# A decoder trunk on one core: the third block sum of each seven-product unit made by an adding transfer instead of by VectorE

## The chip, the cores and the metric

The kernel runs on one core of a Trainium2 chip. The metric is the device time of one execution in microseconds (us), given as the median of several runs. The engines of the core are TensorE (PE in the profile, with its weight loads as PEld), VectorE (DVE), ScalarE (ACT), GpSimd (POOL) and SyncE (SP), and 16 DMA engines move data between the device memory and the on-chip memory.

## The reference

The input is a sequence of 256 tokens of width 1024 in float32. Two layers each do

```python
xn = rms_norm(h, norm_mix_g[layer])
...
h = h + mix
hn = rms_norm(h, norm_ffn_g[layer])
h = h + (silu(hn @ ffn_w_gate[layer]) * (hn @ ffn_w_up[layer])) @ ffn_w_down[layer]
```

The first layer's `mix` is a causal pooling mixer beside differential attention, the second's a convolution module beside block attention. A last RMS norm ends the trunk. `ffn_w_gate` and `ffn_w_up` are 1024 x 2816 and `ffn_w_down` is 2816 x 1024. What matters here is the product of `hn` with the two up matrices.

## The kernel before

**Weights.** Every weight is stored in the device memory as slabs of 128 x 2048 float32 (1 MB). SP loads a slab in two halves (`load`, L488 to L495) into one of five buffers `raw`, or for some slabs into `spare`. The products are made to float32 precision from float32r parts: ACT writes the high part `w_hi` (a copy, L632, or L949 for a slab that is a sum), DVE writes the low part `w_lo = raw - w_hi` (L1120), and PE then runs three matmuls with 512 columns for each 128 x 512 piece: high by high, low input by high weight, high input by low weight. `w_hi` and `w_lo` have six slots (`SLOTS`). A prepared slab may overwrite a slot only when PE has released it (`slab_used`).

**The order.** No scheduler is at work: each engine runs a list that is written out by hand. The function `places` (L81 to L155) sets the order in which slabs are loaded (`loads`) and prepared (`preps`), and which buffer each uses; `next_hi` on ACT and `next_lo` on DVE take the next slab of `preps`.

**The feed-forward stage.** Its 2816 columns are eleven chunks of 256. Six pairs of chunks, at 3, 6 and 8 in each layer (`SEVEN_AT`), are done as seven-product units (Strassen's scheme in Winograd's form), so that seven block products do the work of eight. The four weight blocks of a unit are B11, B12, B21 and B22. Beside B11, B21 and B22 themselves the unit needs four sums of blocks:

- T3 = B12 + B22, held in the buffer y: POOL issues an adding transfer of 1 MB (`add_third`, L600 to L605), which reads B22 from the device memory and adds it into y, where B12 lies. Its semaphore is `third_added`.
- T2 = B11 - T3, held in x, where B11 lay: DVE, `block_add(a, 0)`.
- T1 = T2 + B22, held in y: DVE, `block_add(a, 1)`.
- T4 = T2 + B21, held in x: DVE, `block_add(a, 2)`, with B21 in the buffer e.

All three of DVE are one instruction of 128 x 2048 at L1682, and their semaphore is `block_sum`. A sum may overwrite its buffer only when both parts of what lay there have been taken (`lo_ready` of that slab).

A unit prepares its slabs in the order b11, t3, t2, a down slab, t1, b21, b22, t4, a down slab, and PE uses them in that order (`seven` of the tensor block, L2331 to L2367; a product with a sum is at L2323, L2324 and L2328). Between the products ACT copies partial results out of the PSUM banks (`seven_copy`, L982): the third of these copies reads the result of the t1 product, and PE waits for it before the b22 product. DVE adds it in (`seven_add`, L1690) and, some instructions later, makes the low part of the first turned activation (`seven_act_lo`, L1705), which PE waits for before the down product (L1832 and after).

**POOL.** Its list is short: constants, thirteen small powers for the norms (L615), and after the powers of the feed-forward norm of each layer the three adding transfers of that layer's units, one behind the other.

Of the kernel before, what the change touches and what calls it, by code (L numbers as in the profile page):

```python
# [37 lines left out]
ALU = mybir.AluOpType  # L38
# [24 lines left out]
NAT = (4, 5)  # L63
NCH = 11
SEVEN_AT = ((3, 6, 8), (3, 6, 8))
WHOLE = [("block", l, a + 1, 1) for l in range(2) for a in SEVEN_AT[l]]
SPARE = RAW_SLOTS
EARLY = SPARE + 1

# [11 lines left out]
def places():  # L81

    loads, preps, place = [], [], {}
    counts = [0] * (EARLY + 1)
    freed = {r: (0, []) for r in range(RAW_SLOTS)}
    units = 0

    def load(key):

        n = len(loads)  # L90
        r = min(freed, key=lambda q: freed[q][0])
        _, waits = freed.pop(r)
        counts[r] += 16 if FIRST_SLABS <= n < PARTED else 16 * LOADS
        loads.append((key, r, waits))
        return r, counts[r]

    def prepare(key, r, made):
        place[key] = len(preps)
        preps.append((r, made))

    def free(r, *more):

        freed[r] = (len(preps), [("lo", len(preps))] + list(more))

    def slab(key):
        r, made = load(key)
        prepare(key, r, made)
        if r != EARLY:
            free(r)

    for l in range(2):
        place["mix", l] = len(preps)
        for n in range(NAT[l] + 6):
            slab(("mix", l, n))
        place["out", l] = len(preps)
        for n in range(4):
            slab(("out", l, n))
        spare = [("lo", place["down", 0, NCH - 2] + 1)] if l else []
        for i in range(NCH):
            if i in SEVEN_AT[l]:  # L120
                if i == SEVEN_AT[l][0]:
                    freed[SPARE] = (len(preps) + 1, spare + [("forms", l + 1)])
                x, x_made = load(("block", l, i, 0))
                y, y_made = load(("block", l, i + 1, 0))
                z, z_made = load(("block", l, i + 1, 1))
                d, d_made = load(("down", l, before(l, i)))
                prepare(("b11", l, i), x, x_made)
                prepare(("t3", l, i), y, None)
                prepare(("t2", l, i), x, None)
                prepare(("down", l, before(l, i)), d, d_made)  # L130
                free(d)
                e, e_made = load(("block", l, i, 1))
                place["raw", l, i] = ((x, x_made), (y, y_made), (z, z_made), (e, e_made))
                prepare(("t1", l, i), y, None)
                free(y)
                d, d_made = load(("down", l, i + 1))
                prepare(("b21", l, i), e, e_made)
                prepare(("b22", l, i), z, z_made)
                free(z)
                free(e, ("sum", 3 * units + 3))  # L140
                prepare(("t4", l, i), x, None)
                free(x)
                prepare(("down", l, i + 1), d, d_made)
                free(d)
                units += 1
                continue
            if i - 1 not in SEVEN_AT[l]:
                for n in range(2):
                    slab(("up", l, i, n))
                if i:  # L150
                    slab(("down", l, before(l, i)))
        slab(("down", l, NCH - 1))
        freed.pop(SPARE, None)
        place["end", l] = len(preps)
    return loads, preps, place  # L155
# [13 lines left out]
def trunk(nc, x, x_cols, norm_mix_g, norm_ffn_g, norm_final_g, params_in, slabs, out):  # L169
# [45 lines left out]
    with ctx:  # L215
# [125 lines left out]
        raw_loaded = [sem(f"raw_loaded{i}") for i in range(EARLY + 1)]  # L341
        block_sum = sem("block_sum")
        third_added = sem("third_added")
        low_copied = sem("low_copied")
        x_kept = sem("x_kept")
        forms_made = sem("forms_made")
# [90 lines left out]

            return 4 * (st - 1) + 2 * half + b

        SUMS = ("t2", "t1", "t4")  # L440
        sum_of_prep = {}
        for l in range(2):
            for a in SEVEN_AT[l]:
                sum_of_prep[place["t3", l, a]] = (third_added, 16 * seven_no(l, a) + 16)
                for n, name in enumerate(SUMS):
                    sum_of_prep[place[name, l, a]] = (block_sum, len(SUMS) * seven_no(l, a) + n + 1)
        LOW_AT = [[i for i in range(2, NCH - l) if not in_seven(l, i)] for l in range(2)]
# [39 lines left out]
        def _(sp):  # L487
            def load(n):  # L488

                key, r, free = loads[n]  # L490
                for what, count in free or ():
                    sp.wait_ge({"lo": lo_ready, "forms": forms_ready, "sum": block_sum}[what], count)
                for b in range(2):
                    c = slice(b * SLAB // 2, (b + 1) * SLAB // 2)
                    sp.dma_start(raw_of(r, c), piece(n, c.start, c.stop)).then_inc(raw_loaded[r], 16)  # L495
# [73 lines left out]
        @block.gpsimd  # L569
        def _(pool):  # L570
            made = [0]

            def step(ins):

                made[0] += 1
                ins.then_inc(consts, 1)
                pool.wait_ge(consts, made[0])

            step(nc.gpsimd.memset(power[:, :], -0.5))
            step(nc.gpsimd.memset(ident[:, :], 0.0))  # L580
            step(nc.gpsimd.affine_select(out=ident[:, :], in_=ident[:, :], compare_op=ALU.not_equal, fill=1.0,
                                         base=0, pattern=[[-1, P]], channel_multiplier=1))
            assert made[0] == IDENT_MADE
            step(nc.gpsimd.tensor_copy(ident_b[:, :], ident[:, :]))
            step(nc.gpsimd.memset(mask_b[:, :, :], 0.0))

            step(nc.gpsimd.affine_select(out=mask_b[:, :, :], in_=mask_b[:, :, :], compare_op=ALU.is_ge, fill=NEG,
                                         base=0, pattern=[[0, 4], [-1, P]], channel_multiplier=1))
            pool.wait_ge(cols_lo, KC)


            step(nc.gpsimd.memset(u_in[:, :, 0:UPAD], 0.0))
            for g, w in enumerate(POOL_WINDOWS):
                r = slice(64 * (g % 2), 64 * (g % 2) + 64)
                step(nc.gpsimd.memset(per_count[r, g // 2, :], 1.0 / w))
                for t in range(w - 1):
                    step(nc.gpsimd.memset(per_count[r, g // 2, t:t + 1], 1.0 / (t + 1)))
            assert made[0] == CONSTS_MADE

            def add_third(l, a):  # L600

                y, made = place["raw", l, a][1]
                n = [key for key, _, _ in loads].index(("block", l, a + 1, 1))
                pool.wait_ge(raw_loaded[y], made)
                nc.gpsimd.dma_start(raw_of(y), piece(n, 0, SLAB), accum_op=ALU.add).then_inc(third_added, 16)  # L605

            for n, (kind, a, b) in enumerate(POWS):
                pool.wait_ge(pow_asked, n + 1)
                if kind == "norm":
                    o, i, e = rstd[:, b:b + 1], meansq[:, b:b + 1], power[:, 0:1]  # L610
                elif kind == "head":
                    o, i, e = osq[:, :], osq[:, :], power[:, :]
                else:
                    o, i, e = rstd[:, 2:4], meansq[:, 2:4], power[:, 0:2]
                nc.gpsimd.tensor_tensor(o, i, e, ALU.pow).then_inc(pow_done, 1)  # L615
                if (kind, a, b) in (("norm", 1, 1), ("norm", 3, 1)):
                    for unit in SEVEN_AT[a // 2]:
                        add_third(a // 2, unit)


        @block.scalar
# [484 lines left out]
        def _(dve):  # L1106
# [431 lines left out]
            def ffn_dve(l):  # L1538
# [131 lines left out]
                def block_add(a, m):  # L1670

                    raws = place["raw", l, a]
                    for r, made in ((raws[0],), (raws[2],), (raws[3],))[m]:
                        dve.wait_ge(raw_loaded[r], made)
                    dve.wait_ge(lo_ready, place[("b11", "t3", "t2")[m], l, a] + 1)
                    if m == 0:
                        dve.wait_ge(third_added, 16 * seven_no(l, a) + 16)
                    else:
                        dve.wait_ge(block_sum, 3 * seven_no(l, a) + m)
                    x, y, z, e = (raw_of(r) for r, _ in raws)  # L1680
                    o, p, q = ((x, x, y), (y, z, x), (x, e, x))[m]
                    V.tensor_tensor(o, p, q, ALU.add if m else ALU.subtract).then_inc(block_sum, 1)  # L1682

                def seven_add(a, m):
# [22 lines left out]
                def seven(a):  # L1707
# [3 lines left out]
                    if follows:  # L1711
                        seven_act_lo(a - 2, 3)
                        block_add(a, 1)
                        block_add(a, 2)
                        next_lo()
                    else:
                        next_lo()
                        block_add(a, 2)
                    next_lo(2)
                    if follows:  # L1720
                        seven_add(a, 0)
                        next_lo()
# [778 lines left out]
```

## Time and profile before

| | |
|---|---|
| time of three runs | 559.43, 559.46, 559.73 us; median 559.46 |
| span of the profiled execution | 557.6 us |
| granted clock of TensorE over the span | 0.998 |
| PE, DVE, ACT, POOL busy | 551.2, 467.6, 341.3, 20.4 us |
| adding transfers issued by POOL | 6 of 1 MB |

The profiled execution comes with its span alone, from its first instruction to its last. The median of the timed runs is 1.9 us longer than this span; it is what lies around the span. A matmul's end is modelled in the trace, so PE rows overlap: in a run of matmuls with 512 columns the next one starts every 0.23 us, while each row shows about 0.39 us.

The layers' units stand at these places of the span: unit 3 of layer 0 with its PE products from 146 us, unit 6 from 193 us, unit 8 from 224 us, and in layer 1 from 421, 468 and 499 us.

### The profile page before, as it was taken

Reading aid. Unit: us, or ns where it says so; the run is one execution under the profiler, and the core shown is the slowest. Engines: PE = TensorE matmul, PEld = TensorE weight load, DVE = VectorE, ACT = ScalarE, POOL = GpSimd, SP = SyncE. Lnnn points to the kernel's source line nnn. Section 1 sums busy time; section 2 is a strip of 40 time slices with the busy share of each in tenths; the row PEclk is TensorE's granted clock in tenths of the full one; section 3 lists DMA queues with packets and bytes.
Section 4 is the critical chain, followed back from the end, with each engine's and each line's share of the span. In section 5 each row is a group of like instructions: output and inputs, shape, how many; then the busy total and the mean of one; then the engine's idle time right before and its main releaser. Section 6 shows DMA issues by size and latency. Waiting matters only on the chain.

```text
span 557.6 us, 7496 instructions
## 1 busy us (share of the span) xinstructions
PE 551.2 (99%) x2877; PEld 468.8 (84%) x2877; DVE 467.6 (84%) x562; ACT 341.3 (61%) x471; POOL 20.4 (4%) x60
## 2 busy tenths in 40 slices
PE   9999999999999999999999999999999999999996
PEld 8899988888888888888888888888888888888885
DVE  5779996788996997997798998977889889979875
ACT  6778664756664773666566366647387557656724
POOL 1200001000000000000000000000000000000000
PEclk9999999999999999999999999999999999999999
DMA  8995544474379259277469422444916790773502
GB/s 300 409 401 199 185 150 152 150 216 163 121 277 336 97 182 343 78 285 290 148 253 366 168 75 76 156 147 158 306 64 224 287 320 21 222 286 143 197 1 75
DMA packets 31429, 111.95 MB, mean 201 GB/s; under 512 B 3489, under 2 KB 4641, under 8 KB 30625
## 3 DMA queue, kind: packets, MB, share of 16 engines
q1 hardware_dynamic: 30384, 105.04, 50.2%
q0 software_dynamic: 864, 6.29, 5.8%
q8 instruction: 23, 0.38, 0.3%
q10 hardware_dynamic: 144, 0.14, 0.1%
q14 instruction: 14, 0.11, 0.1%
HBM read 110.40 MB, written 1.05 MB: 200 GB/s over the span
## 4 chain that ended last, share of the span: by engine, by line
PE 99%; DVE 0%; DVEq 0%; issue 0%; ACT 0%; ACTq 0%
PE bank L1834 16%; PE bank L1832 16%; PE bank L1833 16%; PE bank L2277 8%; PE bank L2324 7%; PE bank L2328 7%; PE bank L2323 7%; PE bank L2282 4%; PE bank L1943 4%; PE bank L1946 2%; PE bank L1896 1%; PE bank L1893 1%; PE bank L1889 1%; PE bank L1915 1%; PE bank L2289 1%; PE bank L2035 1%
## 5 line engine op out<-in xcount | busy, mean ns | idle before, releaser
L1120 DVE TENSOR_TENSOR w_lo<-raw,w_hi 128x2048 fp32r<-128x2048 f32 (+2 forms) x98 | 217.2, 2232 | 18.2 <-ACT w_hi L632 16.7
L632 ACT ACTIVATE w_hi<-raw 128x2048 fp32r<-128x2048 f32 (+2 forms) x81 | 149.5, 1861 | 11.4 <-PE bank L1834 7.4
L1832 PE MATMUL bank<-w_lo,yT_hi 128*128 128x512 f32 (+1 forms) x242 | 96.5, 399 | 0.0
L1834 PE MATMUL bank<-w_hi,yT_lo 128*128 128x512 f32 (+1 forms) x242 | 94.1, 389 | 0.0
L1833 PE MATMUL bank<-w_hi,yT_hi 128*128 128x512 f32 (+1 forms) x242 | 94.0, 388 | 0.0
L1834 PEld LDWEIGHTS bank<-w_hi,yT_lo 128*128 128x128 f32 x242 | 45.4, 188 | 9.6
L1832 PEld LDWEIGHTS bank<-w_lo,yT_hi 128*128 128x128 f32 x242 | 45.5, 188 | 8.4 <-DVE yT_lo L1335 0.2
L1833 PEld LDWEIGHTS bank<-w_hi,yT_hi 128*128 128x128 f32 x242 | 45.6, 188 | 8.2
L2277 PE MATMUL bank<-xT,w_hi 128*128 128x512 f32 x192 | 48.5, 394 | 0.0
L949 ACT ACTIVATE w_hi<-raw 128x2048 fp32r<-128x2048 f32 x24 | 45.8, 1910 | 2.9 <-DMA raw<-in_slabs 2.6
L1832 PE MATMUL bank<-w_lo,xT 128*128 128x512 f32 (+1 forms) x112 | 42.8, 382 | 0.0
L1834 PE MATMUL bank<-w_hi,xT 128*128 128x512 f32 (+1 forms) x112 | 42.1, 376 | 0.0
L1833 PE MATMUL bank<-w_hi,xT 128*128 128x512 f32 (+1 forms) x112 | 42.0, 375 | 0.0
L2277 PEld LDWEIGHTS bank<-xT,w_hi 128*128 128x128 f32 x192 | 34.7, 189 | 6.4
L2323 PE MATMUL bank<-w_hi,forms_hi 128*128 128x512 f32 x96 | 37.5, 391 | 0.0
L2324 PE MATMUL bank<-w_hi,forms_lo 128*128 128x512 f32 x96 | 37.4, 390 | 0.0
L1682 DVE TENSOR_TENSOR raw<-raw 128x2048 f32<-128x2048 f32 x14 | 32.0, 2289 | 0.7
L2323 PE MATMUL bank<-w_hi,xT 128*128 128x512 f32 x72 | 28.6, 397 | 0.0
L2324 PE MATMUL bank<-w_hi,xT 128*128 128x512 f32 x72 | 28.1, 390 | 0.0
L2282 PEld LDWEIGHTS bank<-xT,w_lo 128*128 128x128 f32 x192 | 26.2, 190 | 1.9
L1832 PE MATMUL bank<-xT,w_hi 128*128 128x256 f32 x96 | 27.6, 287 | 0.0
L1834 PE MATMUL bank<-xT,w_lo 128*128 128x256 f32 x96 | 27.2, 283 | 0.0
(247 smaller groups left out, 973.3 us busy)
## 6 DMA issues: line engine op xcount, KB each, us to landing
raw<-in_slabs SPq DMA_DIRECT2D x170, 512.0 KB, 4.8
spare<-in_slabs SPq DMA_DIRECT2D x16, 512.0 KB, 7.0
raw<-in_slabs POOLq DMA_DIRECT2D x6, 1024.0 KB, 9.7
raw<-in_slabs SPq DMA_DIRECT2D x5, 256.0 KB, 4.3
h<-in_x SPq DMA_DIRECT2D x2, 512.0 KB, 7.1
early<-in_norm_ffn_g SPq DMA_DIRECT2D x2, 512.0 KB, 10.1
raw<-in_slabs SPq DMA_DIRECT2D x6, 128.0 KB, 4.6
h<-in_x_cols SPq DMA_DIRECT2D x1, 512.0 KB, 5.5
```

What stands on the lines that cost most here:

```text
L632: A(w_hi[:, s % SLOTS, c], raw_of(r, c), ACT.Copy).then_inc(hi_ready, 1)
L949: A(w_hi[:, slot(ahead[0]), :], raw_of(r), ACT.Copy).then_inc(hi_ready, 1)
L1120: V.tensor_tensor(w_lo[:, s % SLOTS, c], raw_of(preps[s][0], c), w_hi[:, s % SLOTS, c].bitcast(F32), ALU.subtract).then_inc(lo_ready, 1)
L1682: V.tensor_tensor(o, p, q, ALU.add if m else ALU.subtract).then_inc(block_sum, 1)
L1832: T.matmul(o, st_hi, mv_lo, start=first, stop=False, skip_group_check=onto)
L1833: T.matmul(o, st_hi, mv_hi, start=False, stop=False, skip_group_check=onto)
L1834: return T.matmul(o, st_lo, mv_hi, start=False, stop=last, skip_group_check=onto)
L2277: T.matmul(bank[:, b + m, :], hi, xT[:, k, :, :, :], start=k == 0, stop=False)
L2282: last = T.matmul(bank[:, b + m, 0:SEQ], lo, xT_hi[:, :, k, :], start=False, stop=k == KC - 1)
L2323: T.matmul(bank[:, b, :], hi[:, k, :], w1, start=not onto and k == 0, stop=False, skip_group_check=onto)
L2324: T.matmul(bank[:, b, :], lo[:, k, :], w1, start=False, stop=False, skip_group_check=onto)
L2328: last = T.matmul(bank[:, b, :], hi[:, k, :], w2, start=False, stop=k == n - 1, skip_group_check=onto)
```

## The change

T4 is no longer made by DVE. POOL gets a second adding transfer for each unit, `add_fourth`: it reads B21 from the device memory and adds it into x, where T2 lies. B21 is now stored in the device memory row by row over its whole width, as B22 is (`WHOLE`), and is still loaded to e for its own product. ACT's high part of T4 waits for `fourth_added`. `block_add(a, 2)` and its place in DVE's list go, and the load that reuses e no longer waits for the sum.

```diff
-WHOLE = [("block", l, a + 1, 1) for l in range(2) for a in SEVEN_AT[l]]
+WHOLE = [("block", l, a + b, 1) for l in range(2) for a in SEVEN_AT[l] for b in range(2)]
...
-                free(e, ("sum", 3 * units + 3))
+                free(e)
...
-        SUMS = ("t2", "t1", "t4")
+        SUMS = ("t2", "t1")
...
+                sum_of_prep[place["t4", l, a]] = (fourth_added, 16 * seven_no(l, a) + 16)
...
+            def add_fourth(l, a):
+
+                x = place["raw", l, a][0][0]
+                n = [key for key, _, _ in loads].index(("block", l, a, 1))
+                pool.wait_ge(lo_ready, place["t2", l, a] + 1)
+                pool.wait_ge(block_sum, len(SUMS) * seven_no(l, a) + 2)
+                nc.gpsimd.dma_start(raw_of(x), piece(n, 0, SLAB), accum_op=ALU.add).then_inc(fourth_added, 16)
...
                         add_third(a // 2, unit)
+                        add_fourth(a // 2, unit)
...
                     if follows:
                         seven_act_lo(a - 2, 3)
                         block_add(a, 1)
-                        block_add(a, 2)
-                        next_lo()
-                    else:
-                        next_lo()
-                        block_add(a, 2)
-                    next_lo(2)
+                    next_lo(3)
```

Two places show how the lists change. The first is DVE in unit 8 of layer 0, where T1 and T4 were made back to back and the low parts of t1, b21 and b22 follow (`raw` and `spare` are the load buffers, `w_lo` the slots). Before:

```order
L1705 TENSOR_TENSOR yT_lo<-bank,yT_hi 128x256 [waits at_hi]
L1682 TENSOR_TENSOR raw<-spare,raw 128x2048 [waits block_sum,lo_ready,raw_loaded5]
L1682 TENSOR_TENSOR raw<-raw 128x2048 [waits block_sum,lo_ready,raw_loaded1]
L1120 TENSOR_TENSOR w_lo<-raw,w_hi 128x2048 [waits hi_ready] x2
L1120 TENSOR_TENSOR w_lo<-spare,w_hi 128x2048 [waits hi_ready]
L1690 TENSOR_TENSOR work<-bank,work 128x512 [waits seven_copied,slab_used]
```

And now:

```order
L1714 TENSOR_TENSOR yT_lo<-bank,yT_hi 128x256 [waits at_hi]
L1691 TENSOR_TENSOR raw<-spare,raw 128x2048 [waits block_sum,lo_ready,raw_loaded5]
L1129 TENSOR_TENSOR w_lo<-raw,w_hi 128x2048 [waits hi_ready] x2
L1129 TENSOR_TENSOR w_lo<-spare,w_hi 128x2048 [waits hi_ready]
L1699 TENSOR_TENSOR work<-bank,work 128x512 [waits seven_copied,slab_used]
```

One sum has left DVE's list and nothing else has moved. The second place is POOL's list in layer 0, from the unit 3 transfer to the next power. Before:

```order
L605 DMA raw<-in_slabs 128x2048 [waits raw_loaded3]
L605 DMA raw<-in_slabs 128x2048 [waits raw_loaded2] x2
L615 TENSOR_TENSOR rstd<-meansq,power 128x1 [waits pow_asked] x2
```

And now:

```order
L605 DMA raw<-in_slabs 128x2048 [waits raw_loaded3]
L613 DMA raw<-in_slabs 128x2048 [waits block_sum,lo_ready]
L605 DMA raw<-in_slabs 128x2048 [waits raw_loaded2]
L613 DMA raw<-in_slabs 128x2048 [waits block_sum,lo_ready]
L605 DMA raw<-in_slabs 128x2048 [waits raw_loaded2]
L613 DMA raw<-in_slabs 128x2048 [waits block_sum,lo_ready]
L623 TENSOR_TENSOR rstd<-meansq,power 128x1 [waits pow_asked] x2
```

The T3 transfer of the next unit now stands behind the T4 transfer of this one, which waits for DVE.

## Rows read from the trace of the kernel before

**Rows 1.** Page, busy us (share of the span) and instructions of each engine

```profile
PE 551.2 (99%) x2877; PEld 468.8 (84%) x2877; DVE 467.6 (84%) x562; ACT 341.3 (61%) x471; POOL 20.4 (4%) x60
```

**Rows 2.** Page, the chain that ended last: shares by engine

```profile
PE 99%; DVE 0%; DVEq 0%; issue 0%; ACT 0%; ACTq 0%
```

**Rows 3.** Waits of PE: engine, line, waited for: us in total, times, longest

```profile
PE bank L1828 <- DVE probT L1802: 1.0, 1, 1.0
```

**Rows 4.** DVE's timeline, unit 8 of layer 0: start, duration, instruction, [idle before]

```profile
229.51 2.29 DVE L1682 TENSOR_TENSOR raw<-spare,raw 128x2048 f32<-128x2048 f32 x1
231.93 2.29 DVE L1682 TENSOR_TENSOR raw<-raw 128x2048 f32<-128x2048 f32 x1
...
241.52 0.69 DVE L1690 TENSOR_TENSOR work<-bank,work 128x512 f32<-128x512 f32 x1
...
247.79 0.42 DVE L1705 TENSOR_TENSOR yT_lo<-bank,yT_hi 128x256 fp32r<-128x256 f32 x1
```

**Rows 5.** ACT's timeline, same unit: the high part of T4, the copy behind

```profile
238.38 1.90 ACT L949 ACTIVATE w_hi<-raw 128x2048 fp32r<-128x2048 f32 x1
240.64 0.60 ACT L982 ACTIVATE work<-bank 128x512 f32<-128x512 f32 x1 [0.35 <-PE bank L2328]
```

**Rows 6.** PE's timeline, same unit: first matmuls of b22 and down product

```profile
243.16 0.39 PE L2323 MATMUL bank<-w_hi,forms_hi 128*128 128x512 f32 x1
...
249.00 0.48 PE L1832 MATMUL bank<-w_lo,yT_hi 128*128 128x512 f32 x1
```

**Rows 7.** Adding transfers of POOL (L605): time from issue to landing

```profile
DMA to landing us min/median/max: 8.9/9.7/10.1
```

**Rows 8.** DMA queue of POOL, packets, MB, share: from 122 to 125 us

```profile
q0 software_dynamic: 78, 0.64, 102.7%
```

**Rows 9.** The same queue from 207 to 210 us, beside transfers of SP

```profile
q0 software_dynamic: 51, 0.42, 71.9%
```

**Rows 10.** Windows: us, PE, PEld, DVE, ACT, POOL busy, PEclk, DMA share, GB/s

```profile
241.52:248.21 6.69, 6.69 (x32) 5.49 (x32) 6.69 (x9) 5.08 (x6) 0.00 (x0) 1.00 0.80 302
205.00:206.50 1.50, 1.50 (x8) 1.27 (x7) 1.50 (x2) 0.76 (x1) 0.86 (x1) 1.00 0.00 0
233.60:238.40 4.80, 4.80 (x23) 3.94 (x22) 4.11 (x3) 4.80 (x4) 0.00 (x0) 1.00 0.03 5
238.60:240.00 1.40, 1.40 (x8) 1.14 (x7) 1.40 (x2) 1.40 (x1) 0.00 (x0) 1.00 0.91 354
```

**Rows 11.** Timelines of DVE, ACT and PE, unit 8 of layer 1

```profile
506.91 2.29 DVE L1682 TENSOR_TENSOR raw<-raw 128x2048 f32<-128x2048 f32 x1
...
513.32 1.90 ACT L949 ACTIVATE w_hi<-raw 128x2048 fp32r<-128x2048 f32 x1
...
523.93 0.48 PE L1832 MATMUL bank<-w_lo,yT_hi 128*128 128x512 f32 x1
```

**Rows 12.** Timelines of DVE and ACT, unit 3 of layer 0

```profile
144.70 2.28 DVE L1120 TENSOR_TENSOR w_lo<-raw,w_hi 128x2048 fp32r<-128x2048 f32 x1
...
154.87 1.92 ACT L949 ACTIVATE w_hi<-raw 128x2048 fp32r<-128x2048 f32 x1 [0.25 <-DVE raw L1682]
...
159.52 1.93 ACT L632 ACTIVATE w_hi<-raw 128x2048 fp32r<-128x2048 f32 x1 [0.93 <-PE bank L1834]
...
162.18 0.60 ACT L982 ACTIVATE work<-bank 128x512 f32<-128x512 f32 x1 [0.73 <-PE bank L2328]
```

**Rows 13.** Timelines of DVE, ACT, POOL: unit 6, and T3, T2 of unit 8

```profile
191.15 2.29 DVE L1120 TENSOR_TENSOR w_lo<-raw,w_hi 128x2048 fp32r<-128x2048 f32 x1
...
202.04 1.91 ACT L949 ACTIVATE w_hi<-raw 128x2048 fp32r<-128x2048 f32 x1
...
207.05 1.92 ACT L632 ACTIVATE w_hi<-raw 128x2048 fp32r<-128x2048 f32 x1 [1.29 <-PE bank L1834]
...
204.99 0.86 POOL L605 DMA_DIRECT2D raw<-in_slabs  x1 [32.48 <-DMA raw<-in_slabs]
...
219.11 2.28 DVE L1682 TENSOR_TENSOR raw<-raw 128x2048 f32<-128x2048 f32 x1
```

More of the change, by code:

```diff
@@ L85, in places @@
     freed = {r: (0, []) for r in range(RAW_SLOTS)}
-    units = 0
     def load(key):
@@ L144, in places @@
                 free(d)
-                units += 1
                 continue
@@ L343, in trunk @@
         third_added = sem("third_added")
+        fourth_added = sem("fourth_added")
         low_copied = sem("low_copied")
@@ L491, in load @@
                 for what, count in free or ():
-                    sp.wait_ge({"lo": lo_ready, "forms": forms_ready, "sum": block_sum}[what], count)
+                    sp.wait_ge({"lo": lo_ready, "forms": forms_ready}[what], count)
                 for b in range(2):
@@ L1672, in block_add @@
                     raws = place["raw", l, a]
-                    for r, made in ((raws[0],), (raws[2],), (raws[3],))[m]:
-                        dve.wait_ge(raw_loaded[r], made)
-                    dve.wait_ge(lo_ready, place[("b11", "t3", "t2")[m], l, a] + 1)
+                    r, made = raws[0] if m == 0 else raws[2]
+                    dve.wait_ge(raw_loaded[r], made)
+                    dve.wait_ge(lo_ready, place[("b11", "t3")[m], l, a] + 1)
                     if m == 0:
@@ L1678, in block_add @@
                     else:
-                        dve.wait_ge(block_sum, 3 * seven_no(l, a) + m)
-                    x, y, z, e = (raw_of(r) for r, _ in raws)
-                    o, p, q = ((x, x, y), (y, z, x), (x, e, x))[m]
+                        dve.wait_ge(block_sum, len(SUMS) * seven_no(l, a) + m)
+                    x, y, z, _ = (raw_of(r) for r, _ in raws)
+                    o, p, q = ((x, x, y), (y, z, x))[m]
                     V.tensor_tensor(o, p, q, ALU.add if m else ALU.subtract).then_inc(block_sum, 1)
```

## The prediction

> **What bounds the kernel now.** I read the busy times first: PE 551.2 us of a span of 557.6, DVE 467.6, and POOL, which gets the new work, 20.4 [rows 1]. Then the chain that ended last, which is PE for 99% and DVE for 0% [rows 2]. Since a busy PE could still be one that waits between matmuls, the list of PE's waits comes next: it holds one wait, of 1.0 us, at the very start of the kernel [rows 3]. So no wait for DVE stands in the 99%, and the question is only whether the new way of T4 puts one in. That is read from the timelines of DVE, ACT and PE around each T4 [rows 4 to 6, 11 to 13], and the duration of the new transfer from the six adding transfers that are there already and from what the DMA engines carry at the time [rows 7 to 10].
>
> **What is removed.** Six sums on DVE of 2.29 us [rows 4], 13.7 us of its 467.6. PE waits for DVE nowhere in the units, so this is worth 0 on the path. Its only trace should be low parts of b21, b22 and t4 made up to 2.3 us sooner in units 3 and 6; the high parts and PE's release of slots set the pace again behind them. SP's wait for the sum goes as well, but its other wait, for b22's low part, comes later than the sum in each unit: 0.
>
> **What is added.** Six transfers of 1 MB, each with this life: POOL issues it when T1 is made (units 8) or when t2's low part is made (units 3 and 6); it lands L us later; ACT, which works in order, takes T4's high part then. I need L and how late T4 may be.
>
> *The length L.* The six existing ones took 8.9 to 10.1 us [rows 7], all beside SP's traffic. With the DMA engines to itself such a transfer moves 0.64 MB in 3 us [rows 8], so 1.05 MB in 4.9 us; beside SP's loads it moves 0.42 MB in 3 us [rows 9], so it would take 7.5 us. Before the first packet there is a start-up: the transfer issued at 204.99 finds idle DMA engines, and nothing moves up to 206.50 [rows 10, 13], so at least 1.5 us; the longest landing less the slow transfer gives at most 10.1 - 7.5 = 2.6. I take 2.0. L lies between 1.5 + 4.9 = 6.4 and the 10.1 of the rows.
>
> The Trainium skill (DMA: Bandwidth & Descriptors, Anatomy of one DMA) puts a transfer issued by GpSimd at about 2.0 us plus its bytes by 436 KB per us. For 1 MB that is an estimate of 4.4 us, by which T4 would land before anyone asks and the sum would be 0 with room to spare; the rows have twice that for an adding transfer, and the rows decide.
>
> *Unit 8 of layer 0, the tight one.* T1 ends at 229.51 + 2.29 = 231.80 [rows 4]; POOL sees it about 0.1 later, as DVE did with its own T4 at 231.93. So the transfer is issued at 231.9, and its packets would run from 233.9. From 233.6 to 238.4 the DMA engines were idle (share 0.03), and at 238.6 SP's next slab begins (share 0.91) [rows 10]. The transfer is alone for 4.7 of its 4.9 us, and the rest at the slow rate costs 0.1 more: landing at about 239.0, **L = 7.1**. ACT asks for T4 at 238.38 [rows 5], so it gets it 0.6 us late.
>
> What stands behind that wait on ACT is the copy of t1's product at 240.64, which had 0.35 us of idle time ahead of it [rows 5]. Behind the copy stands DVE's add at 241.52: the copy ended at 241.24, so with 0.1 for the semaphore about 0.2 us are spare. From 241.52 to 248.21 DVE is busy without a gap [rows 10], up to the end of the low part that starts at 247.79 [rows 4], and PE wants that for its down product at 249.00 [rows 6]: 0.8, less 0.1 for the semaphore, 0.7 spare. Together T4 may be 0.35 + 0.2 + 0.7 = 1.25 us late before PE notices. In terms of L: ACT's request is 6.5 us after the issue, so **PE's stall is L - 7.7 us, and nothing below that**. The direct way, PE's wait for the copy before b22 at 243.16 [rows 6], has more room (copy done at 241.24, 1.8 spare after the 0.35). With L = 7.1 the stall is 0.
>
> *Unit 8 of layer 1.* The same distances: from DVE's old T4 at 506.91 to ACT's request at 513.32 are 6.41 us, and PE's down product follows 10.6 us after that [rows 11], as 10.6 in layer 0. Stall 0.
>
> *Units 3.* T2's low part ends at 146.98, so the issue is at 147.1 and T4 is asked for at 154.87 [rows 12]: 7.8 us. SP's loads come into it half way, so I take L = 8, late by 0.2. Even L = 10.1 makes it only 2.3 late, and ACT idles 0.93 and then 0.73 us for PE before the copy that matters [rows 12]; 0.6 remains, against the 1.8 of the direct way above. Stall 0.
>
> *Units 6.* Issue at 193.44 + 0.1, request at 202.04, 8.5 us; 1.6 late at worst, and 1.29 us of idle time for PE come behind it [rows 13]. Stall 0.
>
> *The queues.* POOL's list is passed in order, so the T3 transfer of the next unit waits for the issue of T4's. That of unit 8 went out at 204.99, when its block had landed [rows 13], and T4's of unit 6 goes out at 193.5: no wait. But T4's transfer takes 5 us of the DMA engines while SP loads that very block, so it lands later; at most some 2.5 us, and T3 is then there near 217, where DVE wants it at 219.11 [rows 13]. The cover is 2 us, and PE's t3 product is several us behind that. SP's own loads get later by as much; what ACT takes behind T4 waits for PE and not for a slab [rows 12, 13]. So 0, and without this cover it would be a stall of 1 to 2 us for each of two units.
>
> **Sum.** 0 removed, 0 added: the span stays at 557.6, and the median of 559.46, which is 1.9 above it, stays at 559.5.
>
> **Rivals.**
>
> *A, late landing (slower).* T4's transfer in units 8 takes as long as those of the rows. Speaking for it: no landing under 8.9 is on record, start-up is bounded only from 1.5 to 2.6, and two transfers in one queue slow each other [rows 8, 9]. Against it: the DMA engines are idle in exactly that stretch [rows 10]. At L = 8.9 each unit 8 stalls 1.2 us, at 10.1 2.4, so 2.4 to 4.8 us in all: **561.9 to 564.3**. It decides from L = 7.7, and can be measured from 8.3 on.
>
> The Trainium skill (same page, Queues, rings and completion order) has the DMA engine change between queues only after a whole packet of some 9 to 17 descriptors. By that a started transfer would hardly be slowed and L would be near 7 everywhere; rows 8 and 9, 26 against 17 packets per us, disagree.
>
> *B, the fall-back of SP and of T3 (slower).* The 6 MB more, 5 us of DMA time each, delay a slab or T3 past its cover. A stall of 1 to 2 us in two units gives **561.5 to 563.5**. It decides from a delay of T3 of over 4 us, the first two of which are DVE's. Against it: the idle times behind T4 in units 3 and 6 end with PE, not with a slab [rows 12, 13].
>
> *C, DVE's relief is worth something (faster).* If small waits under the resolution of the waits list hang on DVE in the units, up to 0.3 us in each could go, 1.8 us: **557.7**. Against it: rows 2 and 3, and ACT rather than DVE stands before PE in the units.
>
> *D, the change does nothing of what it says.* The order of the lists shows that the sum has left DVE and that POOL has six more transfers; I give it nothing.
>
> **How the numbers follow.** The forecast (no stall) 0.74; A 0.17; B 0.05; C 0.04. About 0.2% (1.1 us) is what a measurement of this kernel can tell from no change. A below L = 8.3 stays within that. So faster 0.04, same 0.75, slower 0.21. The range goes from 559.1, a shade of scatter under the fastest of the three runs, to 561.9, the time with the shortest landing that a row shows in both units 8; beyond it lie the longer landings and part of B and C, together under 2 in 10.
>
> **What would show it.** Right: the waits of PE still hold nothing from the units; the landings in units 8 are 7 to 7.6 us, those of units 3 and 6 about 8 to 9; ACT waits 0.3 to 1 us for the transfer at T4 in units 8 and its third copy starts within 0.7 us of where it was; DVE's busy time is 13.7 us less. Wrong: PE idle before the first down matmul (L1832) of units 8, released by DVE's L1705 of before, or before the b22 product (A); ACT or DVE waiting for T3 in unit 8, or for a slab, with PE behind them (B); a span under 556.5 (C).

## The result, and the profile after

| | before | after |
|---|---|---|
| median of five runs each, us | 559.60 | 561.90 |
| lowest and highest of the five | 559.43, 560.21 | 561.71, 562.44 |
| span of the profiled execution | 557.6 | 560.4 |
| ratio of the times, 95% interval | | 1.0042 [1.0030, 1.0055] |

The change makes the kernel 2.3 us slower. The forecast was no change; the time lies at the upper end of the range.

The page of the changed kernel, busy times:

```profile
PE 552.1 (99%) x2874; PEld 467.6 (83%) x2877; DVE 455.1 (81%) x556; ACT 341.0 (61%) x471; POOL 25.7 (5%) x66
```

DVE's busy time fell by 12.5 us [rows 1], for six sums fewer (13.7 by their durations, which overlap their neighbours a little). PE is still 99% busy, so the busy share says nothing of the loss, which is in short idle times. The chain that ended last does: it was PE for 99% before [rows 2], and its largest shares are now DVE 6%, PE 5% and DMA 5% (it is followed back to 459 us of the span and no further). In layer 1 it runs through the transfer of T3, the sum T1, the transfer of T4 and ACT's copy (start, duration, what):

```profile
483.83 12.07 DMA raw<-in_slabs
...
506.52 2.21 DVE raw L1691
...
509.39 8.04 DMA raw<-in_slabs
...
519.27 0.58 ACT work L991
```

The waits of PE (engine, line, waited for: total, times, longest, us) now hold three kinds that were not there [rows 3]:

```profile
PE bank L1832 <- DVE probT L1806: 1.0, 1, 1.0
PE bank L2293 <- DVE work L1706: 0.9, 2, 0.5
PE bank L2327 <- ACT work L991: 0.3, 1, 0.3
PE bank L1998 <- issue: 0.2, 1, 0.2
```

The waits for DVE's L1706 and for ACT's L991 are in the two units 8. The three new kinds add up to 1.4 us, half of the 2.8 us between the spans; the list does not hold all short waits (experiment 4 has stalls of 0.22 us that it leaves out), so I measure the loss below on the starts of instructions. L2293 turns a part of the activation for the down product on PE, right ahead of the first down matmul; L2327 is the b22 product, behind ACT's copy. The timelines there, in layer 0 (start, duration, instruction, [idle before <- what ended it]): ACT,

```profile
236.66 1.91 ACT L641 ACTIVATE w_hi<-spare 128x2048 fp32r<-128x2048 f32 x1
241.26 1.92 ACT L958 ACTIVATE w_hi<-raw 128x2048 fp32r<-128x2048 f32 x1 [2.70 <-DMA raw<-in_slabs]
243.09 0.58 ACT L991 ACTIVATE work<-bank 128x512 f32<-128x512 f32 x1
```

DVE,

```profile
219.98 2.29 DVE L1691 TENSOR_TENSOR raw<-raw 128x2048 f32<-128x2048 f32 x1 [0.71 <-DMA raw<-in_slabs]
...
230.39 2.28 DVE L1691 TENSOR_TENSOR raw<-spare,raw 128x2048 f32<-128x2048 f32 x1
...
243.76 0.69 DVE L1699 TENSOR_TENSOR work<-bank,work 128x512 f32<-128x512 f32 x1 [2.08 <-ACT work L991]
...
250.04 0.42 DVE L1714 TENSOR_TENSOR yT_lo<-bank,yT_hi 128x256 fp32r<-128x256 f32 x1
```

PE,

```profile
243.72 0.50 PE L2327 MATMUL bank<-w_hi,forms_hi 128*128 128x512 f32 x1 [0.31 <-ACT work L991]
...
250.18 0.44 PE L2293 MATMUL bank<-ident,work 128*128 128x128 f32 x2 [0.47 <-DVE work L1706]
250.51 0.50 PE L1836 MATMUL bank<-w_lo,yT_hi 128*128 128x512 f32 x1
```

and POOL's two issues of this unit, that of T3 and that of T4:

```profile
207.41 0.86 POOL L605 DMA_DIRECT2D raw<-in_slabs  x1 [12.56 <-DMA raw<-in_slabs]
233.35 0.89 POOL L613 DMA_DIRECT2D raw<-in_slabs  x1 [25.08 <-DVE raw L1691]
```

Read backwards: the first down matmul comes at 250.51 instead of 249.00 [rows 6], since ACT took T4's high part at 241.26 instead of 238.38 [rows 5]. ACT waited 2.70 us for the transfer. That was issued at 233.35, 0.68 us after T1 had ended (230.39 + 2.28 = 232.67), and landed 7.9 us later. T1 itself was late (229.51 before [rows 4]): DVE waited 0.71 us for T3.

**A common zero.** Executions differ by some tenths of a us before the first unit is reached, and what unit 8 of layer 0 loses shifts all of layer 1. So I measure each layer against a marker ahead of its losses, ACT's high part of the sum at 145 us and its counterpart at 420 us. In the execution before these are

```profile
145.14 1.90 ACT L949 ACTIVATE w_hi<-raw 128x2048 fp32r<-128x2048 f32 x1
...
419.87 1.90 ACT L949 ACTIVATE w_hi<-raw 128x2048 fp32r<-128x2048 f32 x1
```

and in the changed kernel 145.23 and 421.42, shifts of 0.09 and 1.55. By this zero the first down matmul of unit 8 is 250.51 - 249.00 - 0.09 = 1.42 us late in layer 0. In layer 1 it comes at 526.69 instead of 523.93 [rows 11], so it is 1.21 us late. Together that is 2.63 of the 2.8 us between the spans. (The two shifts differ by 1.46 us, which is the loss of layer 0 once more.) The same two differences are taken for every experiment below.

### The profile page after: what moved, and what is told of

It reads as the page before. It is cut to its first block and busy times, and to the rows that moved or that the text cites. A ratio compares the mean times of both kernels' runs of the same rounds, so it can differ in the third digit from the quotient of the medians.

```text
span 560.4 us, 7487 instructions
## 1 busy us (share of the span) xinstructions
PE 552.1 (99%) x2874; PEld 467.6 (83%) x2877; DVE 455.1 (81%) x556; ACT 341.0 (61%) x471; POOL 25.7 (5%) x66
## 3 DMA queue, kind: packets, MB, share of 16 engines
q0 software_dynamic: 1728, 12.58, 11.7%
## 5 line engine op out<-in xcount | busy, mean ns | idle before, releaser
L2327 PE MATMUL bank<-w_hi,forms_hi 128*128 128x512 f32 x96 | 37.8, 393 | 0.4 <-ACT work L991 0.3
L2327 PE MATMUL bank<-w_hi,xT 128*128 128x512 f32 x72 | 28.6, 397 | 0.0
L1836 PE MATMUL bank<-xT,w_hi 128*128 128x256 f32 x96 | 27.6, 287 | 0.0
L1837 PE MATMUL bank<-xT,w_hi 128*128 128x256 f32 x96 | 27.1, 283 | 0.0
```

The source lines that it names most:

```text
L1836: T.matmul(o, st_hi, mv_lo, start=first, stop=False, skip_group_check=onto)
L1837: T.matmul(o, st_hi, mv_hi, start=False, stop=False, skip_group_check=onto)
L2327: T.matmul(bank[:, b, :], hi[:, k, :], w1, start=not onto and k == 0, stop=False, skip_group_check=onto)
```

## The experiments

Two theories were open. *Own latency*: T4's transfer in units 8 is simply too long, by POOL's issue and by its own duration. *Queue*: the transfers and the freed DVE change when T3 of unit 8 lands, and T1 and T4 are late for that. The experiments switch the new way on in some units and not in others, or take away one link. The baseline ran beside them on the same chip: 559.68 us for the first four (29 runs), 559.78 us for the last three (19 runs).

**1. T4 by transfer in units 3 and 6, by DVE in units 8.**

```diff
+BY_POOL = (3, 6)
...
-                        add_fourth(a // 2, unit)
+                        if unit in BY_POOL:
+                            add_fourth(a // 2, unit)
...
+                        if a not in BY_POOL:
+                            block_add(a, 2)
```

> T4 of units 3 and 6 by the adding transfer as in the changed kernel, T4 of unit 8 by DVE as before, so that four transfers of the six are left. Theory (all of the loss is the late T4 in the two units 8): T3 of unit 8 still lands late, near 219.9 us, and T1 ends near 232.7, but DVE's T4 is then made by 235.0 and ACT asks for it at 238.4: no wait of PE in the units, 559.5 us, ratio to before 1.000. Rival (the 6 MB more on the DMA engines, or the transfers of units 3 and 6, cost time by themselves): 560.5 to 561 us, since two thirds of the transfers are there.

Measured: 559.63 us (11 runs), ratio 1.0000 [0.9992, 1.0009]. PE's waits again hold only the 1.0 us at the start, and ACT's high part of T4 and the copy behind it stand as before, with the same 0.35 us:

```profile
238.98 1.91 ACT L970 ACTIVATE w_hi<-raw 128x2048 fp32r<-128x2048 f32 x1
241.24 0.60 ACT L1003 ACTIVATE work<-bank 128x512 f32<-128x512 f32 x1 [0.35 <-PE bank L2351]
```

(This execution has a shift of 0.62; the down matmul is late by -0.02 and 0.00.) In the units that are not in `BY_POOL` all of T4 is as it was, SP's wait for the sum included. What follows: the four new transfers of units 3 and 6 cost nothing by themselves. DVE does wait for T3 in layer 1 here:

```profile
495.29 2.29 DVE L1703 TENSOR_TENSOR raw<-raw 128x2048 f32<-128x2048 f32 x1 [0.57 <-DMA raw<-in_slabs]
```

With T4 made by DVE that wait is harmless too. The queue effect exists without the new way in units 8, and it costs only with it.

**2. T4 by transfer in units 8 alone.** The edit is that of experiment 1 with `BY_POOL = (8,)`.

> T4 of unit 8 alone by the adding transfer, units 3 and 6 by DVE as before. Theory (two causes in a row: T3 late through unit 6's transfer, worth 0.9 us at T1, and then POOL's 0.7 us from T1 to its issue and a transfer of 7.9 us): T3 lands near 214.7, T1 ends at 231.9, the issue is at 232.6, T4 lands at 240.5, 2.0 us after ACT's request. PE's stall is 2.0 - 1.25 = 0.75 us a unit, 1.5 in all: 561.0 us, ratio 1.0027. Rival (unit 6's transfer has nothing to do with it): the full 2.5 to 2.8 us, 562.1.

Measured: 561.25 us (7 runs), ratio 1.0027 [1.0016, 1.0038], 1.6 us over the kernel before. ACT at T4, and POOL's issue:

```profile
240.11 1.92 ACT L970 ACTIVATE w_hi<-raw 128x2048 fp32r<-128x2048 f32 x1 [1.99 <-DMA raw<-in_slabs]
```

```profile
232.11 0.89 POOL L624 DMA_DIRECT2D raw<-in_slabs  x1 [26.64 <-DVE raw L1703]
```

T1 starts at 229.15, on time by the common zero (shift -0.35), and T3 took 9.6 us as before. Still the issue is 0.68 us behind T1's end at 231.43, the transfer takes 8.0 us, and the down matmul is 0.70 late in layer 0 and 0.71 in layer 1. So own latency alone explains 1.4 of the 2.6 us in the traces, 1.6 of 2.3 in the medians.

**3. The fourth sum left out.** No engine makes T4, and the t4 product takes T2 as it lies in x. This part of the computation is missing; DVE is relieved as in the changed kernel, but no new transfer exists.

```diff
-                sum_of_prep[place["t4", l, a]] = (fourth_added, 16 * seven_no(l, a) + 16)
+                sum_of_prep[place["t4", l, a]] = (block_sum, len(SUMS) * seven_no(l, a) + 2)
...
-                        add_fourth(a // 2, unit)
```

> The sum T4 is left out altogether: the t4 product takes T2 in its place, DVE makes no third sum and POOL issues no fourth transfer (the product count stays). Theory (DVE's relief is worth nothing): DVE busy 13.7 us less, no wait of PE in the units, 559.5 us, ratio 1.000. DVE frees unit 6's buffers 2.2 us sooner, so SP's loads stand ahead of the T3 transfer of unit 8, which lands 1 to 2 us later than before but in time. Rival (DVE's relief gains and the transfers take it back): under 558.5 us.

Measured: 559.93 us (11 runs), ratio 1.0001 [0.9992, 1.0010]; the down matmul is on time within 0.03 us in both layers. Taking 13.7 us of work off DVE brings nothing, so rival C is out. B21's new layout in the device memory is in this kernel too, so it costs nothing either. But T3 of unit 8, issued at 205.40, took 12.2 us where it took 9.6. The cause is seen in SP's issues. Before:

```profile
205.72 0.81 SPq L495 DMA_DIRECT2D spare<-in_slabs  x2
206.64 4.52 SPq L495 DMA_DIRECT2D raw<-in_slabs  x6
```

With the sum left out, at a shift of 0.64:

```profile
204.13 0.80 SPq L495 DMA_DIRECT2D spare<-in_slabs  x2
204.98 5.07 SPq L495 DMA_DIRECT2D raw<-in_slabs  x6
```

and in the changed kernel, at a shift of 0.09:

```profile
203.60 0.80 SPq L495 DMA_DIRECT2D spare<-in_slabs  x2
204.45 5.25 SPq L495 DMA_DIRECT2D raw<-in_slabs  x6
```

By the common zero SP's loads start 2.2 us sooner in both, at 203.5 instead of 205.7. In experiment 2, where DVE makes the sum in unit 6, they start at 205.35 + 0.35 = 205.70, as before. SP's loads wait for DVE's low parts; one sum less in unit 6 frees their buffers one sum sooner, and 4 MB of loads then stand beside T3's transfer and partly ahead of it. (SP's wait for the sum went in the same edit, but it isn't the one that counts: the first load is issued 0.03 us behind the low part of b22 both before, at 205.72 after 205.69, and here, at 204.13 after 204.10.)

Where T3 loses the time is seen in the DMA queues. POOL's is q0, SP's is q1. These are the packets, MB and share of the engines from T3's issue on. In the kernel before, over 3.5 us:

```profile
q0 software_dynamic: 30, 0.25, 46.8%
```

With the sum left out, over 4.7 us:

```profile
q1 hardware_dynamic: 347, 1.29, 92.0%
```

Before, T3's first packet starts 1.6 us behind the issue; here it starts 4.8 us behind it, and until then only SP's data moves. From the first packet to the landing it takes 8.0 us before and 7.4 here. So the transfer is not slowed while it runs; it starts later.

**4. ACT's copy ahead of T4's high part in units 8.** The changed kernel with two of ACT's instructions exchanged, so that the copy does not stand behind the wait for the transfer.

```diff
-                        next_hi(4)
+                        next_hi(3)
                         seven_copy(a, 2)
+                        next_hi()
```

> The changed kernel with two entries of ACT's list exchanged in unit 8: the copy of t1's product comes before the high part of T4, so that it no longer stands behind the wait. Theory (the stall comes through ACT's order: T4, then the copy, then DVE's add, then the low part that PE's down product wants): T4 lands at 241.3 as before, its high part ends at 243.2, DVE's low part of it starts at 243.3 in place of 242.1, 1.1 us late against a spare of 0.7: a stall of 0.4 to 0.5 a unit, no wait of PE before the b22 product, 560.4 us, ratio 1.0015. Rival (PE waits for the weights of T4 itself, whatever the order): as the changed kernel, 561.9.

Measured: 560.45 us (11 runs), ratio 1.0013 [1.0004, 1.0023]. The copy waits for PE alone now, T4 comes behind it:

```profile
241.38 0.60 ACT L991 ACTIVATE work<-bank 128x512 f32<-128x512 f32 x1 [2.15 <-PE bank L2333]
241.87 1.91 ACT L958 ACTIVATE w_hi<-raw 128x2048 fp32r<-128x2048 f32 x1
```

The down matmul is late by 0.22 us in each layer, and PE's waits hold only the 1.0 us. In this execution (shifts 0.74 and 1.00) T1 was on time, so the fair comparison is not with 1.42. In layer 0 the transfer was issued at 233.21 and landed 7.95 us later, 2.04 us after ACT's old request, as in experiment 2, where it landed 2.05 us after it and the stall was 0.70. With the copy let past, 0.22 are left: two thirds of a unit's stall came through ACT's order. (In layer 1 it landed 2.43 us late, and 0.22 are left as well.) The rest remains since DVE's low part of T4 still starts 0.95 us later than before, and the low part of the activation stands behind it.

**5. One more instruction of POOL ahead of the issue in units 8.** The changed kernel with a small power of 1.04 us on POOL between T1's semaphore and the issue. `delay_t` is filled once at the start, which raises `delayed` to 1.

```diff
                 pool.wait_ge(block_sum, len(SUMS) * seven_no(l, a) + 2)
+                if a == SEVEN_AT[l][-1]:
+                    nc.gpsimd.tensor_tensor(delay_t[:, :], delay_t[:, :], power[:, :], ALU.pow).then_inc(delayed, 1)
+                    pool.wait_ge(delayed, l + 2)
```

> The changed kernel, and in unit 8 of each layer POOL does one more small power (128 x 4, 1.0 us in the profile before) between T1's semaphore and the issue of T4's transfer. Theory (PE's stall grows one for one with T4's landing, since no spare is left on the path over ACT and DVE): the landing and the stall are 1.0 to 1.1 us later in each layer, 564.0 us, ratio 1.008. Rival (part of the loss is not T4's landing): clearly less than 2 us more than the changed kernel.

Measured: 564.39 us (5 runs), ratio 1.0091 [1.0075, 1.0106]: 4.6 us over the kernel before, where the change alone costs 2.3. POOL:

```profile
232.53 1.04 POOL L616 TENSOR_TENSOR delay_t<-delay_t,power 128x4 f32<-128x4 f32 x1 [24.20 <-DVE raw L1698]
233.99 0.92 POOL L618 DMA_DIRECT2D raw<-in_slabs  x1 [0.43 <-POOL delay_t L616]
```

T1 had ended at 230.09 + 2.29 = 232.38. The power started 0.15 us behind it, while the row of a DMA issue starts 0.42 us after the power that it waited for. So POOL sees the semaphore within 0.15 us, and most of the changed kernel's 0.68 us belongs to the issue. The issue is 1.61 us behind T1's end in place of 0.68. By the common zero (shifts -0.07 and 1.98) ACT takes T4 3.38 us late in layer 0 and 4.24 in layer 1, where it was 2.79 and 2.58 in the changed kernel; the down matmuls are 2.01 and 2.87 late, where they were 1.42 and 1.21. So the added lateness is 0.59 and 1.66 us, and so is the added stall: one for one, as it should be once the spare time is used up. (That the two are not 0.93 each is T1, 0.1 less late here in layer 0 and 0.8 more in layer 1, and the transfer, 0.2 and 0.1 us shorter here.)

**6. By transfer in units 3 and 8.** `BY_POOL = (3, 8)`. **7. By transfer in units 6 and 8.** `BY_POOL = (6, 8)`. These ask which unit's transfer makes T3 of unit 8 late.

> T4 by transfer in units 3 and 8, by DVE in unit 6. Theory (T3 of unit 8 is late through unit 6 alone, whose transfer holds up the block of T3 and whose missing sum on DVE lets SP's loads go ahead of it): T3 lands near 214.5 and T1 ends near 231.5 (before's place), as with unit 8 alone: 561.1 us, ratio 1.0027. Rival (unit 3 has a share in it): nearer to the changed kernel's 561.9.

> T4 by transfer in units 6 and 8, by DVE in unit 3. Theory: all of the changed kernel's loss, T3 of unit 8 lands near 219.9, T1 ends 0.9 us later than before, 561.9 to 562.3 us, ratio 1.0045. Rival: as e6, 561.1.

Measured: 560.87 us (11 runs), ratio 1.0021 [1.0012, 1.0030] without unit 6, and 561.52 us (9 runs), ratio 1.0030 [1.0020, 1.0040] without unit 3. Both are below the changed kernel; their intervals overlap. ACT at T4 in layer 0, experiment 6 and then 7:

```profile
241.13 1.92 ACT L970 ACTIVATE w_hi<-raw 128x2048 fp32r<-128x2048 f32 x1 [1.71 <-DMA raw<-in_slabs]
```

```profile
240.87 1.92 ACT L970 ACTIVATE w_hi<-raw 128x2048 fp32r<-128x2048 f32 x1 [1.88 <-DMA raw<-in_slabs]
```

DVE waits for T3 in neither of the two in layer 0. In layer 1 it waits in experiment 7 alone:

```profile
495.90 2.29 DVE L1703 TENSOR_TENSOR raw<-raw 128x2048 f32<-128x2048 f32 x1 [0.60 <-DMA raw<-in_slabs]
```

The landing of T3 in layer 0, all by the common zero (T2 wants it at 219.11 [rows 13]; T1's lateness is against 229.51 [rows 4] and, in layer 1, 504.50):

| T4 by transfer in | T3 issued | first packet after the issue | landing time | T3 there | T1 late, layer 0 and 1 | down matmul late, 0 and 1 | us over before, from medians |
|---|---|---|---|---|---|---|---|
| none (before) | 204.99 | 1.6 | 9.6 | 214.6 | 0, 0 | 0, 0 | 0 |
| 8 | 204.96 | 1.6 | 9.6 | 214.6 | 0, 0 | 0.70, 0.71 | 1.6 |
| none, sum left out | 204.76 | 4.8 | 12.2 | 216.9 | 0, 0 | 0, 0 | 0.2 |
| 3, 8 | 205.30 | 4.6 | 11.5 | 216.8 | 0, 0 | 0.45, 0.60 | 1.1 |
| 3, 6 | 207.32 | 4.2 | 11.7 | 219.0 | 0.1, 0.6 | 0, 0 | 0 |
| 6, 8 | 207.24 | 4.3 | 11.8 | 219.0 | 0.1, 0.6 | 0.63, 1.07 | 1.7 |
| 3, 6, 8 (the change) | 207.32 | 4.4 | 12.5 | 219.8 | 0.8, 0.4 | 1.42, 1.21 | 2.3 |

I had put some 1 us more on the kernel with 6 and 8 than on that with 3 and 8, and had expected T3 to land at 219.9 with unit 6 and where it did before without it. All three were misses. With 3 and 8 it lands 2.2 us later, though SP's loads start at 205.70 as before. The table shows where: the first packet comes 4.6 us after the issue. T3 and SP's first load are issued close together here. T3 was 0.73 and 0.69 us ahead before, and 0.74 and 0.57 in experiment 2, and its packets started after 1.6 us; with 3 and 8 it was 0.40 and 0.52 ahead, SP's packets came first, and T3's started after 4.6 and 3.4. So a tenth or two of a us in the issue seems to decide over 2 us in the landing. No run sets this distance on purpose, and whether unit 3's transfer or scatter made T3's issue later is open. But this landing stays within DVE's cover. Only with unit 6 by transfer is T3 issued 2.3 us later, since the load of its block stands beside unit 6's T4 transfer, and only then does it reach 219.0, the very edge. The 219.8 of the changed kernel's layer 0 lies within scatter: experiments 4 and 5 run the same lists up to this point, but for a fill at the start of the latter, and T3 lands there at 218.9 and 219.2. At this edge such scatter goes straight into T1.

No version beats the kernel before. Experiments 1 and 3 equal it and nothing is below it, as PE waits for nothing in the units.

## Why the prediction was wrong, and where it was right

It was wrong: PE stalls where rival A said, by A's formula, and a part of rival B joins it. But no landing in units 8 took the 8.9 us on which A's price stood. By L alone, 7.9 to 8.0 us, the formula gives 0.2 to 0.3 us in each unit; that the loss of 2.3 us comes out next to A's lowest price of 2.4 is luck, since POOL's late issue and B's late T1 make up most of it. By the steps:

- **The stall formula** (nothing up to 1.25 us of lateness of T4, one for one beyond) held. ACT took T4 at 241.26 in the changed kernel, 2.79 late by the common zero, and the stall was 1.42: 1.37 spare. Layer 1 and the units 8 of experiments 5, 6 and 7 give 1.36 or 1.37 as well, layer 0 of experiment 2 gives 1.38.
- **POOL's issue was mis-sized.** "POOL sees it about 0.1 later" was taken from DVE behind its own sum. The issue's row stands 0.68 us behind T1's end: 0.6 us too little.
- **L was mis-sized.** The 7.1 us were 2.0 of start-up, 4.9 of transfer and 0.1 for SP's traffic at its end (which add up to 7.0). It was 7.7 to 8.0 in units 8, with one 8.3 (experiment 4, layer 1). The rate was read in the middle of a running transfer [rows 8] and applied to the whole. In experiment 2 the packets come like this (window, then busy us of PE, PEld, DVE, ACT and POOL, granted clock, DMA share, GB/s; before 233.6 the traffic is SP's, not this transfer's):

```profile
233.60:234.10 0.50, 0.50 (x4) 0.42 (x3) 0.00 (x0) 0.50 (x1) 0.00 (x0) 1.00 2.58 262
234.10:234.60 0.50, 0.50 (x4) 0.41 (x3) 0.06 (x1) 0.50 (x2) 0.00 (x0) 1.00 0.00 0
234.60:237.60 3.00, 3.00 (x15) 2.46 (x14) 3.00 (x2) 3.00 (x2) 0.00 (x0) 1.00 0.96 191
```

  The first half us moves 262 GB/s, 0.13 MB or 16 packets of 8 KB; a pause of half a us follows, and then 191 GB/s over 3 us, 0.57 MB or 70 packets. The first packet starts at 233.7, 1.6 us after the issue, where 2.0 were allowed. The 128 packets of the transfer then take 6.0 us, not 4.9, and it lands 0.3 us after the last, for which the text had no term. The lower bound of the text, 6.4 us, rested on the same rate. The Trainium skill (DMA: Bandwidth & Descriptors, Anatomy of one DMA) would give about 4.4 us by an estimate from its figures; this trace disagrees, and so does every one of the adding transfers here.
- **The queue step failed.** It let T3 land at most 2.5 us later, near 217, under a cover to 219.11. The text had the one cause, T4's transfer of unit 6 beside the load of T3's block, at its right size: the issue moved from 204.99 to 207.41. It missed the other. It had the low parts of b21 and b22 made up to 2.3 us sooner, and it had SP waiting for b22's low part, but it put both at 0 and did not join them: SP's loads came 2.2 us sooner, got ahead of T3, and its landing time went from 9.6 to 12.2 us. Experiment 3, which has no new transfer, shows it. Together T3 came 5.2 us later, not 2.5.
- **The sum of the misses.** In layer 0: T4 predicted 0.6 late, plus 0.6 for the issue, 0.8 for the transfer and 0.8 for T1, is 2.8. Less 1.37 that is the stall of 1.42. Own latency gives 1.41 us for both layers (experiment 2), and T1's lateness of 0.79 and 0.38 the other 1.17, together 2.6 of the measured 2.63.
- **Right:** DVE's relief is worth 0 on PE's path (experiment 3). Units 3 and 6 stall nothing (experiment 1), though the landing time there was 8.2 to 8.5 us. The late T3 cost nothing by itself, only where T4's transfer stood behind it.

The chance of 0.17 for rival A was too low for a sum whose margin of 0.6 us, L from 7.1 to 7.7, hung on three terms, each with an error of that size.

## What to carry to other kernels

When a transfer takes over a step, cost its whole life from rows: from the releasing instruction's end to the issue's row, from there to its first packet, and on to the landing, on a transfer of the same kind and never from a rate in its middle. Ask what stands behind the wait in the waiting engine's list: exchanging two instructions of ACT took back two thirds of a unit's stall. And a relieved engine frees buffers sooner. The loads that this lets go can get ahead of another transfer, so follow them to the next landing that has little cover.

## What the runs showed of the hardware

- An adding transfer of 1 MB with the DMA engines nearly to itself landed 7.7 to 8.0 us after the start of its issue's row, once 8.3 (twelve landings in units 8). In all twelve the first packet started 1.6 to 1.7 us after that start, the 128 packets of 8 KB took 5.7 to 6.3 us, and the landing came 0.3 to 0.4 us after the last. Beside SP's loads such a transfer took 8.1 to 12.9 us.
- On POOL a small power started 0.15 us after the instruction of DVE that released it; a DMA issue's row started 0.6 to 0.7 us after DVE's sum, and 0.42 us after a power of POOL itself.
- An adding transfer that was issued while SP's loads were moving waited for its first packet: 4.2 to 4.9 us after the issue in units 8, where it was 1.6 with the DMA engines idle. That is the way from 9.6 to 12.2 us in experiment 3.
- Once it ran, it held its own. In the kernel before, from its first packet to its last, T3's transfer of unit 8 moved 1.04 MB and SP's loads beside it 0.46 MB, and it took 8.0 us from the first packet to the landing, against 7.4 in experiment 3 behind SP's loads and 6.4 for T4 in experiment 2 nearly alone. The Trainium skill (DMA: Bandwidth & Descriptors, Queues, rings and completion order) has an engine change queues only after a whole packet of several descriptors, by which a started transfer would hardly be slowed. These times bear that out in the main. They do not show how the turns are dealt out, nor why the first packet waits.
